# Two transformer blocks on one core: memory norm, keys and values moved from the first stage into the first feed-forward and the attentions of the second block, modulation first, last tiles by halves

## What is computed

```python
def first_block(x, c, ...):
    mod = silu(c) @ w_ada + b_ada                 # 6 x 1024: shift, scale, gate, twice
    h = rmsnorm(x, norm_mix_g) * (1 + sc_m) + sh_m
    q, k, v, qi, ki, wi, u, ga, gb = split(h @ w_in)
    y_attn = sparse_attention(q, k, v, qi, ki, wi) @ w_attn_proj
    y_conv = silu(layernorm(conv31(glu(u)))) @ w_conv_proj
    x = x + g_m * ((sigmoid(ga) * y_attn + sigmoid(gb) * y_conv) @ w_out)
    h = rmsnorm(x, norm_ffn_g) * (1 + sc_f) + sh_f
    a, b = split(h @ w_ffn_in)
    x = x + g_f * ((silu(a) * b) @ w_ffn_out)
    return rmsnorm(x, norm_final_g)

def second_block(x, mem, ...):
    z = rmsnorm(x, norm_mix_g_2) @ w_in_2         # qa ka va qb kb vb ga gb
    ya = diff_attention(rope(qa), rope(ka), va)   # 4 heads, two softmaxes mixed by lambda
    yb = chunk_band_attention(qb, kb, vb)         # 8 heads
    x = x + (sigmoid(ga) * (ya @ w_up_a) + sigmoid(gb) * (yb @ w_up_b)) @ w_out_2
    k, v = split(rmsnorm(mem, norm_mem_g_2) @ w_ckv_2)     # mem: 256 x 1024
    x = x + cross_attention(rmsnorm(x, norm_cross_g_2) @ w_cq_2, k, v) @ w_co_2
    x = x + swiglu(rmsnorm(x, norm_ffn_g_2), w_gate_up_2, w_down_2)
    return rmsnorm(x, norm_final_g_2)
```

## Time and profile before

| | |
|---|---|
| median of 3 runs | 1089.38 us (1087.8 to 1090.3) |
| profiled execution | 1089.24 us |
| its span | 1087.4 us |
| mean granted TensorE clock | 0.933 |
| TensorE busy | 941.7 us, 87% |
| VectorE busy | 649.2 us, 60% |
| ScalarE busy | 481.7 us, 44% |
| GpSimd busy | 27.6 us, 3% |
| read from memory | 176.39 MB, 163 GB/s over the span |
| chain that ended last | TensorE 49%, issue 27%, VectorE 16%, ScalarE 5%, DMA 2% |

### The profile page before, as it was taken

One profiled execution on the slowest core, in us unless ns is written; L12 is line 12 of the kernel. 1 busy time (PEld: TensorE's weight loads), 2 busy tenths in 40 slices (PEclk: granted clock), 3 DMA queues, 4 the chain that ended last, 5 costly groups with the idle time before them and its releaser, 6 DMA issues.

```text
span 1087.4 us, 11958 instructions
## 1 busy us (share of the span) xinstructions
PE 941.7 (87%) x4205; PEld 764.5 (70%) x4205; DVE 649.2 (60%) x1034; ACT 481.7 (44%) x716; POOL 27.6 (3%) x40
## 2 busy tenths in 40 slices
PE   1998997678877999989959989876898999999896
PEld 1877866456766788878848867655676778888785
DVE  1975989997475455555664743444854455555343
ACT  3623544134544455443333445543444455555332
POOL 1110100000000000000000000000000000000000
PEclk9996999699899899999979989888999999999899
DMA  9893974143153555555734542222544055665340
GB/s 345 298 325 118 330 288 168 65 140 107 49 193 127 184 193 190 185 168 194 273 111 132 193 139 78 78 78 77 174 153 157 1 159 190 193 190 176 138 153 39
DMA packets 101542, 178.03 MB, mean 164 GB/s; under 512 B 5222, under 2 KB 51419, under 8 KB 101498
## 3 DMA queue, kind: packets, MB, share of 16 engines
q1 hardware_dynamic: 94682, 151.23, 41.3%
q0 software_dynamic: 6816, 26.22, 6.5%
HBM read 176.39 MB, written 1.05 MB: 163 GB/s over the span
## 4 chain that ended last, share of the span: by engine, by line
PE 49%; issue 27%; DVE 16%; ACT 5%; DMA 2%; SPq 0%; POOL 0%; DVEq 0%; POOLq 0%; ACTq 0%
PE bank L467 12%; PE bank L468 12%; PE bank L469 12%; PE bank L809 5%; DVE conv_out L1495 4%; DVE w_lo L1313 4%; ACT w_hi L973 2%; DVE ada_acc L1377 2%; DMA tap_rows<-in_w_dw 1%; PE bank L510 1%; PE bank L671 1%; DMA ada_raw<-in_w_ada 1%; PE bank L940 1%; PE bank L531 1%; DVE score L1512 1%
## 5 line engine op out<-in xcount | busy, mean ns | idle before, releaser
L1313 DVE TENSOR_TENSOR w_lo<-raw_weights,w_hi 128x1024 fp32r<-128x1024 f32 x277 | 338.0, 1223 | 313.6 <-ACT w_hi L973 312.8
L973 ACT ACTIVATE w_hi<-raw_weights 128x1024 fp32r<-128x1024 f32 x277 | 292.0, 1057 | 373.7 <-PE bank L469 293.7
L467 PE MATMUL bank<-w_hi,a_hi 128*128 128x512 f32 (+1 forms) x928 | 381.1, 411 | 25.8 <-DVE a_lo L1890 5.9
L468 PE MATMUL bank<-w_lo,a_hi 128*128 128x512 f32 (+1 forms) x928 | 371.7, 400 | 0.0
L469 PE MATMUL bank<-w_hi,a_lo 128*128 128x512 f32 (+1 forms) x928 | 371.1, 400 | 0.0
L467 PEld LDWEIGHTS bank<-w_hi,a_hi 128*128 128x128 f32 x928 | 183.2, 197 | 72.4 <-issue 21.9
L469 PEld LDWEIGHTS bank<-w_hi,a_lo 128*128 128x128 f32 x928 | 182.3, 196 | 39.0
L468 PEld LDWEIGHTS bank<-w_lo,a_hi 128*128 128x128 f32 x928 | 183.0, 197 | 35.5 <-issue 0.2
L809 PE MATMUL bank<-w_hi,ff_hi 128*128 128x512 f32 x176 | 57.0, 406 | 6.3 <-DVE hidden_rows L1755 3.2
L809 PE MATMUL bank<-w_hi,ff_lo 128*128 128x512 f32 x176 | 55.6, 398 | 0.0
L809 PE MATMUL bank<-w_lo,ff_hi 128*128 128x512 f32 x176 | 55.6, 398 | 0.0
(11 more groups left out here) (225 smaller groups left out, 724.6 us busy)
## 6 DMA issues: line engine op xcount, KB each, us to landing
raw_weights<-in_w_in SPq DMA_DIRECT2D x40, 1024.0 KB, 5.0
raw_weights<-in_w_ffn_in SPq DMA_DIRECT2D x44, 512.0 KB, 4.3
raw_weights<-in_w_gate_up SPq DMA_DIRECT2D x44, 512.0 KB, 4.2
ada_raw<-in_w_ada POOLq DMA_DIRECT2D x16, 1024.0 KB, 6.3
raw_weights<-in_w_ffn_out SPq DMA_DIRECT2D x9, 1024.0 KB, 4.8
raw_weights<-in_w_down SPq DMA_DIRECT2D x9, 1024.0 KB, 4.8
raw_weights<-in_w_ckv SPq DMA_DIRECT2D x8, 1024.0 KB, 11.7
ada_late<-in_w_ada POOLq DMA_DIRECT2D x8, 1024.0 KB, 6.1
```

Source lines behind the costliest of these rows:

```text
L467: pe.matmul(ps, hi[:, kt, ts], wh, start=start, stop=False)
L468: pe.matmul(ps, hi[:, kt, ts], wl, start=False, stop=False)
L973: act.activation(w_hi[:, q % RING, 0:m], raw[:, b % RAW, half * PIECE:half * PIECE + m], ACT.Copy)\
L1313: dve.tensor_tensor(w_lo[:, q % RING, 0:m], raw[:, b % RAW, half * PIECE:half * PIECE + m], w_hi[:, q % RING, 0:m], ALU.subtract).then_inc ...
```

## The change

- The modulation comes first. x and c are loaded first (c as columns of 128, straight from memory), and the 32 modulation steps run on VectorE without splits between them; six 1 MB blocks of `w_ada` are issued at once, into two more buffers. SP's queue issues the first block of weights only after 16 steps.
- The memory is loaded, its squares taken and its rows turned in the output part of the first feed-forward (16 transpositions in TensorE's 6th piece there). It is not normed ahead: `norm_mem_g_2` is put in as the turned rows are copied to `mem_hi` and `mem_lo`, and the rows' factor as the keys and values are evicted.
- The 16 pieces of `w_ckv_2` now stand with the 16 gate pieces (`MIXED`): one in each of the 16 steps of the band attention, 1 and 2 by turns in the 8 steps of the differential attention (`FILL2`), four behind it. The sigmoid of the gates is no longer taken as a slab is evicted but apart, for both gates, behind the differential attention.
- The last feed-forward runs its last four pieces for row tile 0 first and then for row tile 1, and the last norm, the residuals and the output go by half tiles.

The core of the diff:

```diff
-P_CKV, U_CKV = 0, 0
-P_SMALL, U_SMALL = 16, 4
+P_SMALL, U_SMALL = 0, 0
+MIXED = (("k", 0), ("k", 1), ("a", 0), ("a", 1), ("b", 0), ("b", 1), ("v", 0), ("v", 1))
+FILL2 = (1,) * 16 + (1, 2) * 4
...
@@ sync @@
-        sp.dma_start(mem_rows[:], a["mem_2"]...
+        sp.dma_start(c_cols[:], a["c"].rearrange("o (k p) -> p (o k)", p=P), allow_slow_non_contiguous=True)...
+        sp.dma_start(x[:], a["x"]...
...
+        sp.wait_ge(ada_step, 16)
+        load(0, w2["w_in"].rearrange("(k p) n -> p k n", p=P)[:, :, C_KI:C_U], "small")
...
+        sp.wait_ge(sem["conv_lo"], 2)
+        sp.dma_start(mem_rows[:], a["mem_2"]...
...
@@ tensor @@
         for s in range(4):
-            slab(P_CKV + 4 * s, U_CKV + s, norm=N_MEM if s == 0 else None)
+            pe.wait_ge(ada_step, 8 * (s + 1))
+            for j in range(4):
+                last = pe.matmul(bank[2][:, 4 * s + j:4 * s + j + 1], ada_acc[:, s, j * P:(j + 1) * P], ones[:, 0:1],
+                                 start=True, stop=True)
...
-        def gates(j):
-            piece(P_IN2 + 24 + j, U_IN2 + 6 + j // 4, j % 4, 4, pair=1)
-        attention("b_", qbT, kbT, E_VB, 0, lambda n: gates(n // 2) if n % 2 else None)
+        def mixed_pieces(n):
+            for j in range(filled(n, FILL2), filled(n + 1, FILL2)):
+                mixed_piece(j)
+            if 9 <= n < 13:
+                g = n - 9
...
+        attention("b_", qbT, kbT, E_VB, 0, mixed_pieces)
...
         for n in range(len(DS)):
             d_turn(n)
             if n + 2 < len(DS):
                 d_scores(n + 2)
-            gates(8 + n)
+            mixed_pieces(16 + n)
...
+        for j in range(28, 32):
+            mixed_piece(j)
...
@@ scalar @@
-            if n >= 2:
-                conv(P_IN2 + 34 + n)
-            if n == 5:
-                slab_out(P_IN2 + 35, U_IN2 + 8, E_GB, ACT.Sigmoid, pair=1, scaled=True)
+            mixed_out(16 + n)
+            mixed_weights(16 + n)
             act.wait_ge(*after("d_", "turned", n + 1))
...
+        def mixed_weights(n):
+            conv(P_IN2 + 28 + filled(n - 1, FILL2), FILL2[n - 1] if n else 0)
...
+        gate_sigmoid(E_GB)
+        conv(P_UB, 4)
+        mixed_slab_out(7)
...
+        gate_sigmoid(E_GA)
         conv(P_UA, 4)
```

More of the change, by code:

```diff
@@ L458, in _ @@
         rstd(N_F2)
-        rstd(N_FINAL2)
+        for t in range(TT):
+            pool.wait_ge(sem["final2_mean"], t + 1)
+            pool.tensor_tensor(stat[:, 6 + t:7 + t], stat[:, 4 + t:5 + t], C("half", 0, 1), ALU.pow)\
+                .then_inc(sem["final2_rstd"], 1)
     @block.tensor
```

415 lines of the change are left out of this document (247 added, 168 removed).

## The result

The changed kernel takes **1126.12 us** (median of 4 runs, 1124.1 to 1127.31), the kernel before 1089.84 beside it: ratio 1.033, 95% interval 1.031 to 1.036. The forecast was 1118 with 1098 to 1138.

A forecast was written before the change was run, and what follows sets the result against it. TensorE was taken as busy nearly everywhere, so gains lie only in its idle, low-clock or droppable time. Terms -41.4 + 1.9 + 24.2 + 1.4 + 23.0 + 13.5 + 8.7 - 2.3 = +29.0 gave 1118 us, range 1098 to 1138.

The forecast's parts named there:

- Differential attention, the mechanism: Differential loop: VectorE's mix stands behind splits waiting for the step before's pieces; TensorE idles 4.05 us a step, +23.0 us.
- The clock: Differential attention: TensorE's clock falls after each of eight idle stretches, mean loss 1.7 us, +13.5 us (bounds 0 and 26).
- First stage: Start to first projection piece: modulation first, features wait for ScalarE's split at 42.6, projection at 58.4 us: -41.4 us.
- Rival D: First stage stays slow as 4-byte elements of the c columns delay modulation; 1120 us with 6 us late; chance 0.04.
- Band attention: Sixteen steps with a piece in each: 8.15 us a pair, 71.3 us against 47.1, +24.2 us.
- entry: Entering the differential part: one Copy eviction and one split of both engines join the chain, 7.9 us, +1.4 us.
- gates: From the differential part's last piece to the first of UA: four more pieces and waits, +8.7 us.
- end: After the last matmul: only tile 1 left, by halves, about 7 us in place of 9.2, -2.3 us.
- Rival A (absorbed): Differential steps keep their 5.5 us chain (6.8 with two pieces) as splits catch up; 1079 to about 1085 us; chance 0.14.
- B: Differential attention: the serial chain holds but the clock doesn't fall; 1103 us; chance 0.14.
- C: Differential attention: the low clock lasts through the one-piece steps, or more; 1118 + 8 to + 20 us; chance 0.08.

The follow-up runs named there:

- lag on both: Changed kernel with the differential loop's weight splits one step later on both ScalarE and VectorE: 1094.72 us, ratio 1.006 to the kernel before.
- The reordered start: Changed kernel with features made before the four first projection pieces are split, and turned vectors copied one modulation slab earlier: 1120.42 us, ratio 1.029.
- the filler: Changed kernel with 20 extra unread 256-column matmuls on split operands in each of the first seven differential steps: 1116.55 us, ratio 1.023.

## Why the prediction was right, step by step

- **Differential attention, the mechanism: right.** Seven stretches of 3.05 to 4.14 us, released by VectorE's mix, ScalarE's splits released by TensorE. TensorE was idle for 26.6 us (87.62 - 61.01) where 7 x 4.05 = 28.4 had been summed. VectorE's splits one step later took all of it away but 0.1 us, and the two runs together showed that it has two parts: waiting for the step before (lag on both: 28 us of the part) and, under it, VectorE's wait for ScalarE's split of the same step (16 us more). My text told the first as the reason and carried the second inside the 3.96 us chain. The two numbers aren't a clean split, as the slab evictions still tie the longest wait of the 16 us to TensorE.
- **The clock: right in kind, too small.** +13.5 was summed from pieces alone, at a mean loss of 1.7. TensorE was busy for 61.0 us, and for 43.7 with the same instructions and no idle stretches, in which only the first piece ran slow: 17.3 us, and some 1.8 for that piece, 19 in all. The pieces alone lost about 15 of it, 1.3 to 2.4 a burst, where 1.7 had been taken from three stretches of 2.2 to 4 us. Transpositions and scores also run at half speed (1.23 us for two-tile scores in place of 0.70), the rest of the 19, and the sum had nothing for them. That is the mis-sized term. It makes +5.6, the idle -1.8 and the own work -0.5: the 3.3 us by which 87.6 lies over 84.3. Where the Trainium skill (TensorE: Matmul & The Clock Gate, HAM oscillation) says that bursts with waits between them start cold every time, the trace agrees: 0.50 to 0.60 over all four single pieces. Behind shorter waits other runs differ (last section).
- **First stage: mis-sized by 3.9.** The features were taken to wait for ScalarE's split of the third piece, and they did, but at 46.05 + 1.0 and not at 42.6. The sum of bytes left out the 0.5 MB of the gate bias on POOL's queue, and took the second 1 MB block as landed when the bytes ahead of it and its own had passed, though the third was issued with it; which of the two delayed it more isn't shown. The reduction on TensorE took 6.83 us behind a late turn where I let 12 of its 16 groups run early; that was hidden by the split and would have come next. The reordered start removed both. Much of the 6.83 us was the low clock: in three runs with the same first stage the reduction took 3.7 to 4.0 us, as its matmuls went over on the way from 0.21 us apart to 0.09.
- **Rival D didn't happen.** The columns of c were there at 3.25 us; the issue and its landing, in the view of transfers to 60 us (queue, count, KB, us to landing):

```profile
c_columns<-in_c SPq DMA_DIRECT2D x1, 4.0 KB, 2.5
```

 The packets under 512 B rose by 1064 on the profile's page, and the load has 1024 elements; where the other 40 come from isn't shown. The Trainium skill (DMA: Bandwidth & Descriptors, Rules for kernel authors) says that a last dimension that isn't contiguous becomes one descriptor per element; the count agrees. At 4 KB it cost nothing that is seen, though whether its packets held back the loads issued behind it wasn't tried: the modulation waited for its own first block, to 11.52.
- **Band attention, entry, gates, end: right** within 0.6 us each. In the band attention the size is partly luck. A pair of steps without an eviction took 8.2 us for 8.15, but TensorE was busy for 68.5 of the 71.7 us where I had taken 67, and idle for 3.2 where the loop of splits was to leave 4.3: it is nearly TensorE's own work that fills a pair. And the terms listed for the loop add up to 4.0 to 4.5 a step, from which the 4.30 and 3.85 can't be had exactly. The 8 steps that had no piece weren't idle: 8 more pieces cost 24.6 us, 3.07 each, more than the 2.72 of a piece where TensorE is the limit.
- **Rival A (absorbed)** needed steps under 7 us. It is what the kernel does with one change of order: 5.5 us a step, and 1079. Its price was near by luck (1079 at best, 1079.3 measured with that edit): the part took 43.8 us and not 51, and the band attention stayed 5 us over the 67 that the 1079 counted on. Its condition was right: the splits don't catch up by themselves, and they did only when VectorE's were moved. **B** (the clock holds) is out: the clock's 13 us showed with the filler. **C** (1118 + 8 to + 20) is not out: its condition, the low clock through the one-piece steps, held for eight or more of the 12 matmuls in each of the four and for all 12 in one, and 1126.12 lies at its lower end. The clock cost 19 us, between the 13.5 of the forecast and the 21.5 with which C begins.
- **The range** held the time (1126 in 1098 to 1138). The point was 8 us low, 3.9 of it in the first stage and 3.3 in the differential part; both errors went the same way: bytes and a slow clock were charged to their largest user alone.

## What to carry to other kernels

When work is moved into a pipelined loop, look for each engine at what stands **ahead of the instruction that the bottleneck waits for**, and at the age of what that waits for. A split that consumes another engine's result should stand a step behind that engine's, not in the same one, even when its buffer is free. Idle TensorE stretches cost twice: by their length, and by the clock of whatever follows, short matmuls included. And "more work in the idle slots" is only a gain where the slots are idle for want of work; here they were idle for want of order, and one line of order was worth more than sixteen moved pieces: it alone brings the kernel before to 0.991, and with the pieces moved as well it is 0.991 again.

## What the runs showed of the hardware

- How long TensorE had stood idle doesn't by itself say whether the clock falls. Behind 3 to 5.4 us of idle every burst in the changed kernel's differential part started at 1.2 GHz. With the short filler, pieces behind 0.81 to 1.54 us ran at 1.00 and behind 1.69 and 1.74 us at 0.77. But with both engines' splits later the bursts behind 2.45 us (first window) and 1.71 us ran at 1.00, and that behind 2.65 us (second window) at 0.77, where it fell only 1 us after TensorE had started again. With VectorE's alone, behind the part, it was 2.18 us at 1.00 and 2.41 us at 0.77. No run shows what decides between these.

```profile
721.29:727.87 6.58, 6.58 (x30) 5.11 (x31) 0.85 (x1) 3.47 (x8) 0.00 (x0) 1.00 0.41 154
736.16:743.51 7.35, 7.35 (x26) 5.94 (x27) 0.00 (x0) 1.07 (x2) 0.00 (x0) 0.77 0.30 114
```

- The record of the clock is wrong at the start of some traces. The small product (48 matmuls of 72 columns) and what follows it, first in the changed kernel, then with only VectorE's splits later, which changes nothing in this stage:

```profile
52.12:62.35 10.23, 10.23 (x48) 10.23 (x49) 2.13 (x2) 0.00 (x0) 0.00 (x0) 1.00 0.33 104
62.35:67.00 4.65, 4.65 (x15) 3.76 (x16) 2.37 (x3) 1.45 (x4) 0.00 (x0) 1.00 0.16 28
```

```profile
52.29:62.52 10.23, 10.23 (x48) 10.23 (x49) 2.12 (x2) 0.00 (x0) 0.00 (x0) 0.50 0.33 104
62.52:67.67 5.15, 5.15 (x13) 4.09 (x14) 2.38 (x3) 1.30 (x3) 0.00 (x0) 0.50 0.25 56
```

 The same product takes 10.23 us in both, recorded at 1.00 in one and at 0.50 in the other, and the 512-column matmuls behind it start 0.43 us apart in both, the pace at a recorded 0.50 everywhere else. So the 1.00 of the changed kernel is not its clock there. The second run differs in that its reduction of the modulation sped up on the way (4.04 us in place of 6.83, as in two other runs) and that a fall to 0.50 was recorded when it ended. In the kernel before, the product took 10.43 us at a recorded 0.50. So all of these products ran at the low level, and no run shows what 72 columns take at the high one.
- A matmul of 256 columns on plain 32-bit operands took 0.44 us (10.5 us for 24; the trace has two records for each), on the split operands 0.13 (2.6 us for 20).
